# Opening of a two-layer encoder kernel: all token tiles loaded at once, remainders shared between two engines, projections begun between the transpositions

## The chip, the cores and the metric

One core of a Trainium2 chip runs the whole program. Its engines work through lists of their own and meet only at semaphores: TensorE (PE in the rows, its weight loads PEld), VectorE (DVE), ScalarE (ACT), GpSimd (POOL), and SyncE (SP), which here only issues DMAs. The metric is the device time of one execution in microseconds, lower is better.

## What is computed

A sequence of 1024 tokens of width 1024 goes through two layers, each a norm, a mixer and a residual. The change lies in the first norm and the start of the first projection:

```python
def rms_norm(x, g):
    xf = x.astype(jnp.float32)
    y = xf * lax.rsqrt(jnp.mean(xf * xf, axis=-1, keepdims=True) + EPS)
    return (y * g.astype(jnp.float32)).astype(x.dtype)

def attention_mixer(hn, w_in, sink, w_out):
    proj = hn @ w_in
    ...
    o = windowed_gqa_sink(q, k, v, sink)
    o = (o * jax.nn.silu(gate.astype(jnp.float32))).astype(hn.dtype)
    return o @ w_out

def reference(x, attn_norm, attn_w_in, ...):
    ...
    for i in range(DEPTH):
        p = layer_params[i]
        hn = rms_norm(x, p[0])
        if i % N_MIXERS == 0:
            x = x + attention_mixer(hn, *p[1:])
        else:
            x = x + deltanet_mixer(hn, *p[1:])
    return rms_norm(x, final_norm)
```

Everything is float32. The kernel gets near that precision with a rounded type: each operand is a rounded part (`_hi`) and a remainder (`_lo`), and a product is three matmuls, hi by hi, hi by lo and lo by hi.

## The kernel before

**Tokens** are cut into eight tiles of 128 (`NT`), the width into eight slices of 128 (`KT`). A token tile t goes through a chain over four engines, and `layer0_order` names its steps:

- `sq`: ScalarE squares the tile and sums the squares (L1037). It writes the squares into `xn`, a double buffer, so it waits until the transpositions of tile t-2, which used the same buffer, are done (`xT_done`).
- `nrm`: VectorE forms the mean (L1306), ScalarE takes the root (L1044), VectorE takes the reciprocal and multiplies the tile by it (L1308, L1309).
- `ntr`: TensorE transposes it in two halves of four 128x128 pieces into banks 4 and 5 (even t) or 6 and 7 (odd t) (L1750).
- `nout`: VectorE multiplies each half by the norm's weights into `hn_plain` (L1317).
- `nhi`: ScalarE rounds it into `hn_hi` (L1050).
- `nlo`: GpSimd subtracts, into `hn_lo` (L949).

**Weight tiles** of the projection (128 columns of `w_in`, 512 KB each) come into `ring0`; `rnd` rounds one on ScalarE (L1072), `split` forms its remainder on GpSimd (L955).

**Projections.** Tokens are taken in two halves of 512. An item `proj` is one slice of the width for one weight tile and one half: three matmuls of 128x512 (L1765). The first 16 items (48 matmuls) are two weight tiles on the first half, token tiles 0 to 3. The first of them waits until eight `nlo` are done (`hn_done`) and the first remainder is there; item 17, which works on the second half, waits for all sixteen. From then on the projections of the first layer run between the attention blocks, in one long stream.

**What sets the order.** `layer0_order` writes one list by hand (`AEV`), and each engine runs those of its events in that order, one after the other. An event that waits holds up everything behind it on its engine. `fill(n)` puts the next n projection items at that place. Before the change the loop of L375 puts tile t's `sq`, `nrm`, `ntr`, then `nout` of tile t-1, then `nhi` and `nlo` of tile t-2; four items stand between the transpositions of tiles 6 and 7 and the other twelve behind those of tile 7.

**Loads.** `xr` holds three token tiles (`XR`), so SyncE waits from tile 3 on until a buffer has been read (L810 to L829).

Of the kernel before, what the change touches and what calls it, by code (L numbers as in the profile page):

```python
# [21 lines left out]
F32 = mybir.dt.float32  # L22
F32R = mybir.dt.float32r
I32 = mybir.dt.int32
ALU = mybir.AluOpType
ACT = mybir.ActivationFunctionType
AX = mybir.AxisListType

P = 128
SEQ, D = 1024, 1024  # L30
NT = SEQ // P
# [16 lines left out]
XR = 3  # L48


def hybrid_encoder_kernel(nc, x, w0, wout0, w1, wba, wout1, norm0, norm1, normf, sink, convw, alog, dtb, onorm, out):
    ctx = ExitStack()
    with ctx:
# [7 lines left out]
        ident = sb("ident", [P, P])  # L61
        g0 = sb("g0", [P, KT])
# [60 lines left out]
        xr = take([XR, D])  # L123
# [14 lines left out]
        def hn_part(t, hf):  # L138
            return hn_f[:, 4 * hf:4 * hf + 4, t * P:(t + 1) * P]
# [207 lines left out]
        def layer0_order():  # L347
# [18 lines left out]
            def fill(n):  # L366
                for _ in range(min(n, len(stream))):
                    put(*stream.pop(0))
# [5 lines left out]
            stream += first + rest  # L374
            for t in range(NT):  # L375
                put(("sq", 0, t), ("nrm", 0, t), ("ntr", 0, t, 0), ("ntr", 0, t, 1))
                if t >= 1:
                    put(("nout", 0, t - 1, 0), ("nout", 0, t - 1, 1))
                if t >= 2:
                    for hf in range(2):  # L380
                        put(("nhi", 0, t - 2, hf), ("nlo", 0, t - 2, hf))
                if t < 2:
                    put(("rnd", t), ("split", t))
                if t >= 6:
                    fill(4 if t == 6 else 0)
            put(("nout", 0, NT - 1, 0), ("nout", 0, NT - 1, 1))
            for t in (NT - 2, NT - 1):
                for hf in range(2):
                    put(("nhi", 0, t, hf), ("nlo", 0, t, hf))
            put(("dist",))  # L390
# [106 lines left out]
        def xr_of(layer, t):  # L497

            if layer == 0:
                return xr[:, t % XR]  # L500
            return xr[:, (OP_SEQ.index((0, t)) if t < XR else NT + t - XR) % XR]
# [24 lines left out]
        def wout_lo(j):  # L526

            if j < 4:
                return hn_lo[:, 2 * j:2 * j + 2, 0:HALF]
            return wout_late_lo[:, j - 4].rearrange("p (f n) -> p f n", f=2)  # L530

        AEV = layer0_order()
# [271 lines left out]
        def _(sp):  # L804

            sp.dma_start(g0[:], norm0).then_inc(ld_g0, 16)
            for t in range(2):
                sp.dma_start(xr[:, t, :], x[:, t, :]).then_inc(ld_x[t], 16)
            sp.dma_start(ring0[:, 0], w0[0, 0]).then_inc(ld_w[0], 16)
            sp.dma_start(xr[:, 2, :], x[:, 2, :]).then_inc(ld_x[2], 16)  # L810
            sp.dma_start(ring0[:, 1], w0[0, 1]).then_inc(ld_w[1], 16)
            for t in range(XR, NT):
                sp.wait_ge(xn_done, t - XR + 1)
                sp.dma_start(xr[:, t % XR, :], x[:, t, :]).then_inc(ld_x[t], 16)
                if t == XR:
                    sp.dma_start(sinkb, sink.partition_broadcast(P)).then_inc(ld_small, 16)
                    sp.dma_start(wba_s, wba).then_inc(ld_small, 16)
                    sp.dma_start(g1[:], norm1).then_inc(ld_small, 16)
                    sp.dma_start(onw[:], onorm).then_inc(ld_small, 16)
                    sp.dma_start(cw[:], convw).then_inc(ld_small, 16)  # L820
                    sp.dma_start(alb[:], alog.partition_broadcast(P)).then_inc(ld_small, 16)
                    sp.dma_start(dtbb[:], dtb.partition_broadcast(P)).then_inc(ld_small, 16)
                if t == XR + 1:
                    for i in range(2):
                        sp.wait_ge(w0_split, i + 1)
                        sp.dma_start(ring0[:, i], w0[0, 2 + i]).then_inc(ld_w[i], 16)
            for tile in range(4, A_GROUPS * W0_TILES):
# [99 lines left out]
        def _(pool):  # L927
# [14 lines left out]
            for e in AEV:  # L942
                if e[0] == "nlo":

                    layer, t, hf = e[1:]
                    q = 2 * (NT * layer + t) + hf
                    tok, ks = slice(t * P, (t + 1) * P), slice(4 * hf, 4 * hf + 4)
                    pool.wait_ge(hi_done, q + 1)
                    gp.tensor_tensor(hn_lo[:, ks, tok], hn_part(t, hf), hn_hi[:, ks, tok].bitcast(F32),  # L949
                                     ALU.subtract).then_inc(hn_done, 1)  # L950
                elif e[0] == "split":

# [70 lines left out]
        def _(act):  # L1023
            sc = nc.scalar

            for e in AEV:
                if e[0] == "sq":
# [259 lines left out]
        def _(dve):  # L1287
# [12 lines left out]
            for e in AEV:  # L1300
                if e[0] == "nrm":

                    layer, t = e[1:]
                    n = NT * layer + t
                    dve.wait_ge(sq_done, n + 1)
                    ve.tensor_scalar(stat[:, 1, t:t + 1], stat[:, 0, t:t + 1], 1.0 / D, EPS, ALU.mult, ALU.add).then_inc(ms_done, 1)  # L1306
                    dve.wait_ge(rt_done, n + 1)
                    link(ve.reciprocal(stat[:, 2, t:t + 1], stat[:, 2, t:t + 1]))  # L1308
                    ve.tensor_scalar(xn_of[layer][:, t % 2], xr_of(layer, t), stat[:, 2, t:t + 1], None, ALU.mult).then_inc(xn_done, 1)  # L1309
                elif e[0] == "nout":  # L1310

# [828 lines left out]
```

## Time and profile before

| | us |
|---|---|
| median of 3 runs | 1339.96 |
| lowest, highest | 1338.75, 1340.84 |
| the profiled execution | 1342.17 |
| its span in the trace | 1340.5 |
| TensorE busy in the span | 1270.4 (95%) |

The span runs from the first to the last instruction in the trace; the execution's own time is 1.67 us longer, and lies 2.21 us above the median of the three runs. A row of the timeline gives the start and the duration of a group of instructions that follow each other, then engine, line, operation, output<-input and the count, and in brackets how long the engine sat idle before it and what released it. The page prints TensorE's granted clock as full over the opening; at which of its two levels (1.2 and 2.4 GHz) it ran is seen better in how far apart the starts of equal matmuls are.

### The profile page before, as it was taken

The page shows a single profiled execution, that of the slowest core. Times are in us where ns is not written, and L with a number is a line of the kernel's source. Part 1 is how long each engine was busy: PE and PEld are TensorE (multiplying, and loading weights), DVE is VectorE, ACT ScalarE, POOL GpSimd, SP SyncE. Part 2 cuts the span into 40 slices and gives each one's busy share as a digit, 9 for nine tenths or more (in the row PEclk, how much of TensorE's full clock was granted, in tenths as well). Part 3 has the DMA queues.
Part 4 walks back from the last instruction along what each step waited for, and adds up shares of the span by engine and source line. Part 5 has one row for each costly group of instructions (what it writes and reads, how often), then busy time and mean ns, then how long its engine had stood idle before and what let it go on. Part 6 is the DMA issues. An engine that isn't in the chain of part 4 may idle for free.

```text
span 1340.5 us, 23647 instructions
## 1 busy us (share of the span) xinstructions
PE 1270.4 (95%) x8829; PEld 973.2 (73%) x8829; DVE 852.6 (64%) x2340; ACT 691.8 (52%) x1806; POOL 278.3 (21%) x188
## 2 busy tenths in 40 slices
PE   5999999999999999878999999999999999998997
PEld 4866766666667776667888888888888888865643
DVE  5334545444656545786897978879788797852343
ACT  6245465464564444535557485574856647552121
POOL 7220111020232244204104031040310403100000
PEclk9999999999999989888999999999999999999999
DMA  5111101011322231111011111110201101053111
GB/s 195 33 32 32 33 32 32 17 32 64 126 69 89 79 126 64 49 33 49 32 33 64 33 52 45 53 60 17 79 18 65 48 18 64 1 221 110 48 68 74
DMA packets 21761, 79.94 MB, mean 60 GB/s; under 512 B 3216, under 2 KB 3472, under 8 KB 20240
## 3 DMA queue, kind: packets, MB, share of 16 engines
q1 hardware_dynamic: 21648, 78.42, 17.0%
q8 instruction: 72, 1.18, 0.4%
q14 instruction: 41, 0.34, 0.1%
HBM read 63.66 MB, written 14.75 MB: 58 GB/s over the span
## 4 chain that ended last, share of the span: by engine, by line
PE 75%; DVE 11%; ACT 9%; issue 2%; DMA 2%; SPq 0%; POOL 0%; DVEq 0%; POOLq 0%
PE bank L1865 19%; PE bank L1765 17%; PE bank L1841 6%; PE bank L1905 4%; PE bank L1880 4%; PE bank L1792 4%; DVE arena L1504 3%; PE bank L1803 3%; PE bank L1818 3%; PE bank L1957 2%; PE bank L1964 2%; PE bank L1990 2%; PE bank L1938 2%; PE bank L1939 2%; PE bank L1950 2%
## 5 line engine op out<-in xcount | busy, mean ns | idle before, releaser
L1865 PE MATMUL bank<-hn_hi,w_hi 128*128 128x512 f32 x512 | 222.5, 435 | 0.5 <-ACT arena L1147 0.5
L1865 PE MATMUL bank<-hn_hi,w_lo 128*128 128x512 f32 x512 | 202.5, 395 | 0.0
L1865 PE MATMUL bank<-hn_lo,w_hi 128*128 128x512 f32 x512 | 201.4, 393 | 0.0
L1765 PE MATMUL bank<-hn_hi,w_hi 128*128 128x512 f32 x320 | 137.0, 428 | 0.5 <-ACT arena L1082 0.2
L1765 PE MATMUL bank<-hn_hi,w_lo 128*128 128x512 f32 x320 | 126.1, 394 | 0.0
L1765 PE MATMUL bank<-hn_lo,w_hi 128*128 128x512 f32 x320 | 125.8, 393 | 0.0
L1003 POOL TENSOR_TENSOR w_lo<-arena,w_hi 128x1024 fp32r<-128x1024 f32 x24 | 59.9, 2495 | 301.6 <-ACT w_hi L1178 301.6
L1113 ACT ACTIVATE arena<-bank 128x512 f32<-128x512 f32 x88 | 52.2, 598 | 118.0 <-PE bank L1803 118.0
L1865 PEld LDWEIGHTS bank<-hn_hi,w_lo 128*128 128x128 f32 x512 | 96.8, 189 | 22.1
L1363 DVE CUSTOM_DVE_ANT_0 arena<-bank,arena 128x384 f32<-128x384 f32 (+1 forms) x128 | 70.1, 581 | 63.7 <-issue 63.4
L1865 PEld LDWEIGHTS bank<-hn_hi,w_hi 128*128 128x128 f32 x512 | 97.6, 191 | 16.2 <-ACT arena L1147 0.7
L1865 PEld LDWEIGHTS bank<-hn_lo,w_hi 128*128 128x128 f32 x512 | 98.0, 191 | 12.4
L955 POOL TENSOR_TENSOR w_lo<-arena,w_hi 128x1024 fp32r<-128x1024 f32 x20 | 48.0, 2399 | 266.7 <-ACT w_hi L1072 266.6
L1504 DVE SCALAR_TENSOR_TENSOR arena<-arena,cw 128x1024 f32<-128x1024 f32 x72 | 101.8, 1413 | 1.2
L1765 PEld LDWEIGHTS bank<-hn_hi,w_hi 128*128 128x128 f32 x320 | 60.7, 190 | 32.2 <-issue 22.8
L1104 ACT ACTIVATE arena<-arena 128x384 f32<-128x384 f32 (+1 forms) x128 | 73.5, 578 | 1.6 <-DVE arena L1372 1.4
L1164 ACT ACTIVATE arena<-bank,arena 128x128 f32<-128x128 f32 x112 | 41.4, 370 | 62.8 <-PE bank L1950 62.8
L1765 PEld LDWEIGHTS bank<-hn_hi,w_lo 128*128 128x128 f32 x320 | 60.5, 189 | 13.2
L1478 DVE SCALAR_TENSOR_TENSOR arena<-bank,arena 128x128 f32<-128x128 f32 x256 | 68.1, 341 | 2.0 <-ACT arena L1190 1.7
L1765 PEld LDWEIGHTS bank<-hn_lo,w_hi 128*128 128x128 f32 x320 | 61.0, 191 | 8.4
L1880 PE MATMUL bank<-arena 128*128 128x512 f32 x120 | 59.5, 624 | 5.7 <-DVE arena L1602 2.9
L1382 DVE TENSOR_SCALAR arena<-arena 128x384 f32<-128x384 f32 (+1 forms) x128 | 60.4, 536 | 1.1
(258 smaller groups left out, 2744.4 us busy)
## 6 DMA issues: line engine op xcount, KB each, us to landing
arena<-in_w SPq DMA_DIRECT2D x52, 512.0 KB, 3.5
arena<-in_x SPq DMA_DIRECT2D x16, 512.0 KB, 4.6
arena<-gc_scratch SPq DMA_DIRECT2D x8, 1024.0 KB, 4.8
x_scratch<-arena SPq DMA_DIRECT2D x13, 512.0 KB, 2.6
arena<-x_scratch SPq DMA_DIRECT2D x13, 512.0 KB, 3.5
out<-arena SPq DMA_DIRECT2D x8, 512.0 KB, 2.6
oT_scratch<-arena SPq DMA_DIRECT2D x7, 512.0 KB, 5.3
arena<-oT_scratch SPq DMA_DIRECT2D x7, 512.0 KB, 7.8
```

Source lines behind the costliest of these rows:

```text
L1003: gp.tensor_tensor(w_lo[:, t % 2], ring1[:, t % 2], w_hi[:, t % 2].bitcast(F32), ALU.subtract).then_inc(w_split, 1)
L1104: sc.activation(pr[:, sl, 0:w], pr[:, sl, 0:w], ACT.Exp, bias=small0[:, HPG + hd:HPG + hd + 1], accum_out=small0[:, 3 * HPG + hd:3 * HPG + ...
L1363: ve.tensor_tensor_reduce(out=pr[:, sl, 0:w], in0=s_bank(hd)[:, 0:w], in1=bias[:, hd, off:off + w], scale=1.0, scalar=small0[:, 7 * HPG + ...
L1382: ve.tensor_scalar(pr[:, sl, 0:w], pr[:, sl, 0:w], small0[:, 5 * HPG + hd:5 * HPG + hd + 1], None, ALU.mult).then_inc(p_norm, 1)
L1478: ins = ve.scalar_tensor_tensor(wq[:, d, c, part], bank_of[:, cc * P:(cc + 1) * P], head_tab2[:, h % 2, 7, u:u + 1], ET[:, d, c], ALU.mult ...
L1504: link(ve.scalar_tensor_tensor(dst, src, tap, dst, ALU.mult, ALU.add))
L1765: ins = te.matmul(bank[r % 2][:], wp[:, tile % 2, k], hp[:, k, hf * HALF:(hf + 1) * HALF], start=(k == 0 and m == 0), stop=(k == KT - 1 an ...
L1792: te.matmul(s_bank(hd)[:, 0:P * len(kt)], qT[rows, g % 2, pair, n * P:(n + 1) * P], kz[g % 2][rows, kt[0] * P:(kt[-1] + 1) * P], start=Tru ...
L1841: ins = te.matmul(bank[u % 2][:], op, wp, start=(j == 4 * part and m == 0), stop=(j == 4 * part + 3 and m == 2))
L1865: ins = te.matmul(b[:], wp[:, t % 2, k], hp[:, k, hf * HALF:(hf + 1) * HALF], start=(k == 0 and m == 0), stop=(k == KT - 1 and m == 2))
L1880: ins = te.matmul(bank[u % 2][:], oT_e[:, j, t * P:(t + 1) * P], wout_e[:, j, hf * HALF:(hf + 1) * HALF], start=(j == 0), stop=(j == FIN_H ...
L1905: ins = te.matmul(fin_bank(w)[:], oT_e[:, j, t * P:(t + 1) * P], wout_e[:, j, hf * HALF:(hf + 1) * HALF], start=(j == first), stop=(j == K ...
```

## The change

- **Loads:** SyncE issues all eight token tiles at the start without waits, tiles 0 and 1 first, then the norm's weights and the first weight tile, tiles 2 and 3, the second weight tile, tiles 4 to 7. Tiles 3 to 7 lie in `oT`, which is not in use yet. The small tables follow, then the third and fourth weight tile.
- **Order:** the hand-written list of the opening is new. `sq` of tiles 2 and 3 stand ahead of `nout` of tiles 0 and 1; tiles 2 and 3 get `nout`, `nhi`, `nlo` directly; three projection items then stand ahead of the transpositions of tile 4, two ahead of tile 5's, one each ahead of tile 6's and 7's. From tile 4 on `nhi` and `nlo` of tile t-1 stand directly behind its `nout`, ahead of `sq` of tile t+1.
- **Remainders:** VectorE does the remainders of the first two weight tiles and of the second halves of tiles 2 and 3; GpSimd keeps the other fourteen `nlo`. Ahead of its seventh it waits for all eight of the first half.
- **Mean:** on VectorE the step of L1306 follows `sq` in the list instead of opening `nrm`, so it stands ahead of `nout`.
- **Root table:** ScalarE takes a root of a constant first.

```diff
+            for t in range(2):
+                put(("sq", 0, t), ("nrm", 0, t), *two("ntr", t))
+            put(("sq", 0, 2), ("rnd", 0), *two("nout", 0), ("nrm", 0, 2), *two("ntr", 2), *two("nhi", 0), *two("nlo", 0))
+            put(("sq", 0, 3), *two("nout", 1), ("nrm", 0, 3), *two("ntr", 3), *two("nhi", 1), *two("nlo", 1), ("split", 0))
+            put(("sq", 0, 4))
+            for t in (2, 3):
+                put(*two("nout", t), *two("nhi", t), *two("nlo", t))
+            put(("rnd", 1), ("nrm", 0, 4), ("split", 1))
+            fill(3)
+            put(*two("ntr", 4))
+            for t in range(5, NT):
+                put(("sq", 0, t), ("nrm", 0, t))
+                fill(2 if t == 5 else 1)
+                put(*two("ntr", t), *two("nout", t - 1), *two("nhi", t - 1), *two("nlo", t - 1))
+            put(*two("nout", NT - 1), *two("nhi", NT - 1), *two("nlo", NT - 1))
...
             if layer == 0:
-                return xr[:, t % XR]
+                return xr[:, t] if t < XR else oT[:, t - XR]
...
+        def lo_by_dve(layer, t, hf):
+
+            return layer == 0 and t in (2, 3) and hf == 1
...
+            for t in range(NT):
+                sp.dma_start(xr_of(0, t), x[:, t, :]).then_inc(ld_x[t], 16)
+                if t == 1:
+                    sp.dma_start(g0[:], norm0).then_inc(ld_g0, 16)
+                    sp.dma_start(ring0[:, 0], w0[0, 0]).then_inc(ld_w[0], 16)
+                if t == 3:
+                    sp.dma_start(ring0[:, 1], w0[0, 1]).then_inc(ld_w[1], 16)
...
                     pool.wait_ge(hi_done, q + 1)
+                    if q == NT:
+                        pool.wait_ge(hn_done, NT)
...
-                elif e[0] == "split":
+                elif e[0] == "split" and e[1] >= 2:
...
+            act.wait_ge(consts, 1)
+            sc.activation(stat[:, 5, 0:1], ident[:, 0:1], ACT.Sqrt)
...
-                if e[0] == "nrm":
+                if e[0] == "sq" and e[1] == 0 or e[0] == "nrm" and e[1] == 1:
...
+                elif e[0] == "split" and e[1] < 2:
```

VectorE from the reciprocal of tile 3 on. Before the change (each row an instruction of L1306 to L1317):

```order
L1308 RECIPROCAL stat<-stat 128x1 [waits rt_done]
L1309 TENSOR_SCALAR arena<-arena,stat 128x1024 [waits dch]
L1317 TENSOR_TENSOR hn_plain_51<-bank4,g0 128x4x128 [waits xT_done]
L1317 TENSOR_TENSOR hn_plain_51<-bank5,g0 128x4x128 [waits xT_done]
L1306 TENSOR_SCALAR stat<-stat 128x1 [waits sq_done]
```

And with it, where L1332 is the weight remainder, L1340 `nout` and L1326 the remainder of a half tile:

```order
L1319 RECIPROCAL stat<-stat 128x1 [waits rt_done]
L1320 TENSOR_SCALAR arena<-arena,stat 128x1024 [waits dch]
L1332 TENSOR_TENSOR w0_lo_53<-arena,w0_hi_52 128x1024 [waits w0_rounded]
L1313 TENSOR_SCALAR stat<-stat 128x1 [waits sq_done]
L1340 TENSOR_TENSOR hn_plain_51<-bank4,g0 128x4x128 [waits xT_done]
L1340 TENSOR_TENSOR hn_plain_51<-bank5,g0 128x4x128 [waits xT_done]
L1326 TENSOR_TENSOR hn_lo_50<-hn_plain_51,hn_hi_49 128x4x128 [waits hi_done]
L1340 TENSOR_TENSOR hn_plain_51<-bank6,g0 128x4x128 [waits xT_done]
L1340 TENSOR_TENSOR hn_plain_51<-bank7,g0 128x4x128 [waits xT_done]
L1326 TENSOR_TENSOR hn_lo_50<-hn_plain_51,hn_hi_49 128x4x128 [waits hi_done]
```

Three subtractions have come in between the multiplication of tile 3 and the end of tile 3's `nout`, and the mean of tile 4 stands ahead of tile 2's `nout`.

ScalarE for tiles 5 to 7 before the change, where L1037 is `sq`, L1044 the root and L1050 `nhi` (two halves each, the last row six halves):

```order
L1037 ACTIVATE arena,stat<-arena 128x1024 [waits xT_done,ld_x6]
L1044 ACTIVATE stat<-stat 128x1 [waits ms_done]
L1050 ACTIVATE hn_hi_49<-hn_plain_51 128x4x128 [waits half_done] x2
L1037 ACTIVATE arena,stat<-arena 128x1024 [waits xT_done,ld_x7]
L1044 ACTIVATE stat<-stat 128x1 [waits ms_done]
L1050 ACTIVATE hn_hi_49<-hn_plain_51 128x4x128 [waits half_done] x6
```

And with it (L1044, L1051 and L1057 are the same three steps):

```order
L1044 ACTIVATE arena,stat<-arena 128x1024 [waits xT_done,ld_x6]
L1051 ACTIVATE stat<-stat 128x1 [waits ms_done]
L1057 ACTIVATE hn_hi_49<-hn_plain_51 128x4x128 [waits half_done] x2
L1044 ACTIVATE arena,stat<-arena 128x1024 [waits xT_done,ld_x7]
L1051 ACTIVATE stat<-stat 128x1 [waits ms_done]
L1057 ACTIVATE hn_hi_49<-hn_plain_51 128x4x128 [waits half_done] x4
```

The rows look alike, but the two `nhi` ahead of `sq` of tile 7 are those of tile 4 before the change and those of tile 5 with it: six halves are left over at the end before, four with it.

TensorE with the change, from the first projection item to the transpositions of tile 6 (L1773 is a transposition, L1788 a projection):

```order
L1788 MATMUL bank0<-hn_hi_49,w0_hi_52 128x512 [waits hn_done,w0_split]
...
L1773 MATMUL bank4<-ident,arena 128x128 [waits half_done,xn_done]
L1773 MATMUL bank4<-ident,arena 128x128 x3
L1773 MATMUL bank5<-ident,arena 128x128 [waits half_done,xn_done]
L1773 MATMUL bank5<-ident,arena 128x128 x3
L1788 MATMUL bank0<-hn_hi_49,w0_hi_52 128x512
...
L1773 MATMUL bank6<-ident,arena 128x128 [waits half_done,xn_done]
L1773 MATMUL bank6<-ident,arena 128x128 x3
```

Before the change the first projection item stands behind the transpositions of tile 6, so that one tile is left to transpose behind it; now four are.

## Rows read from the trace of the kernel before

**Rows 1.** The page's first part: busy time and share of the span.
```profile
PE 1270.4 (95%) x8829; PEld 973.2 (73%) x8829; DVE 852.6 (64%) x2340; ACT 691.8 (52%) x1806; POOL 278.3 (21%) x188
```

**Rows 2.** Stages: window, length, then each engine's busy time (count), clock, DMA share, GB/s.
```profile
0.00:28.49 28.49, 13.41 (x57) 11.04 (x57) 17.20 (x51) 20.20 (x39) 21.22 (x22) 1.00 0.68 229
28.49:42.27 13.78, 13.78 (x58) 11.35 (x57) 8.48 (x13) 3.91 (x7) 8.83 (x7) 1.00 0.01 2
```

**Rows 3.** Timeline of TensorE around the first projection items.
```profile
26.87 1.97 PE L1750 MATMUL bank<-ident,arena 128*128 128x128 f32 x8 [0.94 <-DVE arena L1309]
28.49 0.78 PE L1765 MATMUL bank<-hn_hi,w_hi 128*128 128x512 f32 x1
...
32.05 0.63 PE L1765 MATMUL bank<-hn_hi,w_lo 128*128 128x512 f32 x1
...
33.29 1.04 PE L1750 MATMUL bank<-ident,arena 128*128 128x128 f32 x8
```

**Rows 4.** The chain that ended last, its longest pieces: start, duration, what.
```profile
34.33 13.63 PE bank L1765 x60
```

**Rows 5.** Timeline of tile 5's norm; last, tile 7 on its way to GpSimd.
```profile
21.34 1.06 ACT L1037 ACTIVATE arena<-arena 128x1024 f32<-128x1024 f32 x1 [1.31 <-DMA arena<-in_x]
...
22.53 0.15 DVE L1306 TENSOR_SCALAR stat<-stat 128x1 f32<-128x1 f32 x1 [0.92 <-ACT arena L1037]
...
23.15 0.75 DVE L1309 TENSOR_SCALAR arena<-arena,stat 128x1024 f32<-128x1024 f32 x1
...
23.96 1.97 PE L1750 MATMUL bank<-ident,arena 128*128 128x128 f32 x8 [1.53 <-DVE arena L1309]
...
33.93 1.29 DVE L1317 TENSOR_TENSOR hn_plain<-bank,g 128x512 f32<-128x512 f32 x2 [3.00 <-PE bank L1750]
...
34.66 1.23 ACT L1050 ACTIVATE hn_hi<-hn_plain 128x512 fp32r<-128x512 f32 x2 [3.06 <-DVE hn_plain L1317]
```

**Rows 6.** Timeline: SyncE's first token load; ScalarE's table load in tile 0.
```profile
1.23 0.89 SPq L808 DMA_DIRECT2D arena<-in_x  x2
...
6.14 1.28 ACT L1044 ACT_TABLE_LOAD   x1
```

**Rows 7.** DMA issues between 1.1 and 1.5 us: count, size, us to landing.
```profile
arena<-in_x SPq DMA_DIRECT2D x1, 512.0 KB, 3.7
```

**Rows 8.** The same between 3.0 and 3.4 us, the fifth large load.
```profile
arena<-in_w SPq DMA_DIRECT2D x1, 512.0 KB, 7.1
```

**Rows 9.** Timeline of VectorE beside GpSimd's remainders, tile 3 and tile 7.
```profile
16.30 1.19 DVE L1309 TENSOR_SCALAR arena<-arena,stat 128x1024 f32<-128x1024 f32 x1
...
16.90 1.73 POOL L949 TENSOR_TENSOR hn_lo<-hn_plain,hn_hi 128x512 fp32r<-128x512 f32 x1
...
35.37 1.29 POOL L949 TENSOR_TENSOR hn_lo<-hn_plain,hn_hi 128x512 fp32r<-128x512 f32 x1 [0.76 <-ACT hn_hi L1050]
...
35.45 1.48 DVE L1323 TENSOR_TENSOR wba_lo<-arena,wba_hi 128x256 fp32r<-128x256 f32 x1
```

**Rows 10.** Groups of VectorE by shape: busy us, mean ns, idle before.
```profile
L1581 DVE TENSOR_TENSOR arena<-arena 128x512 f32<-128x512 f32 x16 | 10.3, 688 | 11.7 <-ACT arena L1237 11.7
L1511 DVE TENSOR_TENSOR w_lo<-arena,w_hi 128x1024 fp32r<-128x1024 f32 x6 | 7.1, 1182 | 0.0
```

**Rows 11.** Timeline of TensorE behind three of its idle gaps later in the program.
```profile
378.75 0.33 PE L1803 MATMUL bank<-ident,arena 128*128 128x128 f32 x1 [1.74 <-DVE arena L1382]
...
379.39 0.39 PE L1841 MATMUL bank<-hn_lo,oT_hi 128*128 128x512 f32 x1
...
477.19 0.79 PE L1841 MATMUL bank<-w_hi,oT_hi 128*128 128x512 f32 x1 [3.09 <-DVE arena L1401]
...
478.63 0.63 PE L1841 MATMUL bank<-w_hi,oT_hi 128*128 128x512 f32 x1
...
1192.30 4.51 PE L1880 MATMUL bank<-arena 128*128 128x512 f32 x6 [2.80 <-DMA arena<-oT_scratch]
...
1197.81 1.98 PE L1880 MATMUL bank<-arena 128*128 128x512 f32 x4
```

More of the change, by code:

```diff
@@ L374, in layer0_order, with two @@
             stream += first + rest
[L375 to L389, printed above, removed]
+            def two(what, t):
+                return [(what, 0, t, hf) for hf in range(2)]
+            for t in range(2):
[13 more added lines that the diff above has]
+            put(*two("nout", NT - 1), *two("nhi", NT - 1), *two("nlo", NT - 1))
             put(("dist",))
@@ L804, in _ @@
         def _(sp):
[L806 to L826, printed above, removed]
@@ new lines, in _ @@
+            for t in range(NT):
[5 more added lines that the diff above has]
+                    sp.dma_start(ring0[:, 1], w0[0, 1]).then_inc(ld_w[1], 16)
+            sp.dma_start(sinkb, sink.partition_broadcast(P)).then_inc(ld_small, 16)
+            sp.dma_start(wba_s, wba).then_inc(ld_small, 16)
@@ new lines, in _ @@
+            sp.dma_start(g1[:], norm1).then_inc(ld_small, 16)
+            sp.dma_start(onw[:], onorm).then_inc(ld_small, 16)
+            sp.dma_start(cw[:], convw).then_inc(ld_small, 16)
+            sp.dma_start(alb[:], alog.partition_broadcast(P)).then_inc(ld_small, 16)
+            sp.dma_start(dtbb[:], dtb.partition_broadcast(P)).then_inc(ld_small, 16)
+            for i in range(2):
+                sp.wait_ge(w0_split, i + 1)
+                sp.dma_start(ring0[:, i], w0[0, 2 + i]).then_inc(ld_w[i], 16)
@@ L942, in _ @@
             for e in AEV:
-                if e[0] == "nlo":
+                if e[0] == "nlo" and not lo_by_dve(*e[1:]):
                     layer, t, hf = e[1:]
@@ L1306, in _ @@
                     ve.tensor_scalar(stat[:, 1, t:t + 1], stat[:, 0, t:t + 1], 1.0 / D, EPS, ALU.mult, ALU.add).then_inc(ms_done, 1)
+                if e[0] == "nrm":
+                    layer, t = e[1:]
+                    n = NT * layer + t
                     dve.wait_ge(rt_done, n + 1)
@@ L1309, in _ @@
                     ve.tensor_scalar(xn_of[layer][:, t % 2], xr_of(layer, t), stat[:, 2, t:t + 1], None, ALU.mult).then_inc(xn_done, 1)
+                elif e[0] == "nlo" and lo_by_dve(*e[1:]):
+                    layer, t, hf = e[1:]
+                    tok, ks = slice(t * P, (t + 1) * P), slice(4 * hf, 4 * hf + 4)
+                    dve.wait_ge(hi_done, 2 * t + hf + 1)
+                    ve.tensor_tensor(hn_lo[:, ks, tok], hn_part(t, hf), hn_hi[:, ks, tok].bitcast(F32),
+                                     ALU.subtract).then_inc(hn_done, 1)
+                elif e[0] == "split" and e[1] < 2:
+                    tile = e[1]
+                    dve.wait_ge(w0_rounded, tile + 1)
+                    ve.tensor_tensor(w0_lo[:, tile], ring0[:, tile], w0_hi[:, tile].bitcast(F32), ALU.subtract).then_inc(w0_split, 1)
                 elif e[0] == "nout":
```

## Prediction, written before the changed kernel ran

> **What bounds the kernel now.** I read the page first: TensorE is busy for 95% of the span [rows 1], so whatever it loses or gains is the kernel's time. Then the stages: up to its first projection matmul at 28.49 us TensorE is busy for only 13.41 us, from there on without a gap [rows 2]. The opening is thus worth looking at, and two moments matter. The first is the start of the projections, S: 28.49. The second is the end of the first 48 matmuls (16 items), E. Behind E the order is the same in both kernels, so the change is worth what E moves, as long as the second half of the tokens is ready by then. In the timeline [rows 3] the reader sees eight transpositions (tile 6), then matmuls whose records last 0.63 us, up to 32.05, then eight transpositions in 1.04 us instead of 1.97 (tile 7). The chain of waits shows 60 matmuls in 13.63 us, 0.227 each [rows 4]. So TensorE is at its lower level (1.2 GHz) at first, though the page prints the granted clock as 1.00 there: the 12 matmuls and the way to tile 7's transpositions take 33.29 - 28.49 = 4.8 us, 0.40 each, where 12 x 0.227 = 2.7 would do. The piece of 60 begins at 34.33 with the second matmul behind tile 7, so that E = 34.33 + 35 x 0.227 = 42.3, or S + 13.8.
>
> What E must cover is easily counted: 48 matmuls x 0.227 = 10.9, plus about 2 for the slow beginning, plus 1.0 for each tile that is still to be transposed behind S. Before, that is one tile; with the change it is four. So even without any wait E = S + 17: **the change has to bring S forward by 3 us only to break even.** The second view to read is then the chain of a tile, step by step [rows 5].
>
> **The chain of a tile.** From `sq` to the first transposition: 21.34 to 22.53 (square to mean), to 23.15 (root, reciprocal), to 23.96: 2.6 us. From there the transpositions need about 1.1 us (at the lower level) until VectorE can begin `nout` of the first half. From `nout` to `nhi` is 34.66 - 33.93 = 0.73, and ScalarE is free again after the two `nhi`, 1.2 later. GpSimd's subtraction begins 35.37 - 34.66 = 0.71 after `nhi` [rows 5, 9].
>
> **Part 1, the start S.** The loads first. The first token tile was issued at 1.23 and landed 3.7 later, at 4.9 [rows 6, 7]; the fifth large load, issued at about 3.1, landed 7.1 later, at 10.2 [rows 8]: four transfers of 512 KB in 5.3 us, 1.3 each. With the change the first is issued at about 0.80, in the place of the norm's weights, and lands at 4.5; the ten large loads then land in their order every 1.3 us, the last near 16.3. No tile from the second on is waited for by my count, so the loads give 0.4. The table load of 1.28 that stands in tile 0's chain [rows 6] is done while ScalarE waits for tile 0. Together tile 0's multiplication ends at 4.5 + 2.6 = 7.1 instead of 8.6.
>
> From there I replay the four engines' lists with the durations above:
> - tile 0 is transposed from 7.1 to 8.9, tile 1 to 10.3; `sq` of tile 2 can start at 9.0, since it needs tile 0's buffer. VectorE has nothing to do from 8.6 to 10.2, because the mean of tile 2 now stands ahead of tile 0's `nout`, ready since 8.3. Then `nout` of tile 0 (2 x 0.6), and tile 2's multiplication ends at 12.5. Before, it ended at 14.6: 2.1 gained.
> - `sq` of tile 3 starts at 12.3, VectorE again waits for it until 13.5, does `nout` of tile 1, and starts tile 3's multiplication at 15.1; it ends at 15.8.
> - now the subtractions on VectorE. Alone they cost 1.18 for a weight tile and 0.69 for a half tile [rows 10]. Beside GpSimd they cost more: the subtraction of 256 columns at 35.45 took 1.48 us, and it ended just 0.27 after GpSimd's of 35.37 had (35.37 + 1.29 = 36.66); a multiplication that takes 0.75 alone took 1.19 there, and GpSimd's next, 1.73 instead of 1.27 [rows 5, 9]. I take it that the one that starts first makes the other wait for nearly its whole length. GpSimd starts the remainder of tile 1 when VectorE's multiplication ends, so the weight remainder waits for about 1.0 and ends at 17.95.
> - mean of tile 4, `nout` of tile 2 from 18.05; `nhi`; GpSimd has the first half from 19.5 to 20.7, VectorE's half waits for that until 20.5 and ends at 21.2; the same for tile 3: `nout` from 21.15, GpSimd 22.6 to 23.8, VectorE to 24.3. Eight remainders are there, and S = 24.4 to 24.5, **4.0 us ahead of 28.49**.
>
> So four remainders taken from GpSimd pay for themselves, but of the about 3.7 us that they cost VectorE alone (2 x 1.18 + 2 x 0.69) a part and 2.0 us of waiting stand in front of S.
>
> **Part 2, from S to E.** Three items at the lower level (the ninth matmul started 3.56 after the first [rows 3]) take about 3.8, then tile 4 is transposed at S + 3.8 = 28.2. From here on the new order binds. `sq` of tile 6 stands behind `nhi` of tile 4 on ScalarE, and that one needs tile 4's transpositions: 1.1 (to `nout`) + 0.73 + 1.2 = 3.0, then 2.6 to the transpositions of tile 6: 28.2 + 5.6 = 33.9. `nout` of tile 5 stands behind tile 6's multiplication on VectorE, then `nhi` of tile 5, then `sq` of tile 7: 1.9 + 2.6, less 0.1 that overlaps, 4.4: tile 7's transpositions start at 38.3. Before, a tile came every 2.9 us there (23.96, 26.87), because `nhi` of the tile two back was long ready when its turn came. TensorE has only one item between tiles 6 and 7, 0.7 us, and so it stands idle for 4.4 - 1.0 - 0.7 = 2.7 us ahead of tile 7, and for 1.3 ahead of tile 6. Behind tile 7 come its 1.0 and nine items of 3 x 0.227: 7.1. E = 38.3 + 7.1 = 45.4 if TensorE stays at the higher level.
>
> Does it? After a gap of 1.74 the matmul record behind lasts 0.39; after 3.09 it is 0.63, and after 2.80 six matmuls take 4.51, 0.75 each, where 0.50 is usual a little later (4 in 1.98) [rows 11]. The gap of 2.7 is nearest to the one of 2.80, so I take the lower level again. That costs what it cost at the start, 4.8 - 2.7 - 0.2 for the seam = 1.9, here rounded down to 1.8, since the transpositions are part of it: **E = 47.2 instead of 42.3, +4.9 us.**
>
> GpSimd ends its sixteenth remainder at about 44.5, 0.9 ahead of E even in the faster case, so the second half is not waited for. The loads of the third and fourth weight tile wait for the remainders at 18.0 and 26.3 and are used much later; the copies behind `dist` on VectorE have several us of room. They cost nothing; if GpSimd were over 2.7 us later, item 17 would wait for it.
>
> **The sum.** S -4.0; three more tiles behind S, +3.1 (3 x 1.04); waits of TensorE between the items, 1.3 + 2.7 = 4.0; the second slow stretch +1.8. Together +4.9. The profiled execution's 1340.5 would be 1345.4 in its span; the runs' median is 1339.96, so 1344.9.
>
> **Rivals.**
> 1. *TensorE keeps the higher level over the gap.* For it: the gap of 1.74 did. Then +3.1, 1343.1.
> 2. *VectorE loses the race at tile 3.* Its multiplication is ready at 15.07 and GpSimd's first remainder of tile 1 at 15.08 by my count, a tie. If GpSimd is first, the multiplication waits for 1.1 and all behind it moves: +6.0, 1346.0. The rows show such waits in both directions [rows 9]. The Trainium skill says it as a rule (SBUF — State Buffer, "Who interferes with whom"): issue order decides which of the two blocks, and the other blocks fully. By that rule the tie at tile 3 is worth the 1.1, and the rows agree.
> 3. *The subtractions on VectorE do not wait for GpSimd.* The only such row is one of 256 columns. Without any waits my replay has S at 22.5 and all behind it 2.0 sooner. With the slow stretch E is +2.9, without it +1.1: **no measurable change**, 1341.1. It decides itself at tile 7's transpositions: they must start before about 37.9 for E to stay within 2.7 of 42.3 at the higher level.
> 4. *The tiles come at their old pace of 2.9.* Then tile 7 starts at 28.2 + 8.7 = 36.9 and E = 44.0, +1.7, no measurable change. Against it stands ScalarE's list. Rivals 3 and 4 together would give 42.1, no gain either: for a clear gain S would have to be under 22.
>
> **How the numbers follow.** A difference of 0.2% (2.7 us) is about what a measurement of this kernel can tell from none. Forecast as worked out 0.38; rival 1 0.20; rival 2 (with or without the second slow stretch) 0.14; rival 3 0.12; rival 4 0.10; something faster that the rows do not show, an earlier S by over 3 us, 0.06. Rivals 3 and 4 and a little of rival 1, which lies just over the bound, make no measurable change: 0.25. Faster 0.06, slower 0.69. The range goes from rival 3 without the slow stretch to rival 2 with it and a little: 1340.8 to 1346.8.
>
> **What would show it.** First projection matmul near 24.5. VectorE's weight remainder at about 2.2 us, two thirds of it waiting. TensorE's transpositions of tiles 4, 6, 7 near 28.2, 33.9 and 38.3, with a gap of about 2.7 ahead of the last and records of 0.63 behind it; item 17 near 47.2. If tile 7 comes at 36 or sooner, my reading of ScalarE's order is wrong; if S comes after 26, it is the waits between VectorE and GpSimd or the loads.

## Result and profile of the changed kernel

| | before | changed |
|---|---|---|
| median | 1339.81 us (4 runs, 1338.75 to 1340.84) | 1347.93 us (4 runs, 1347.44 to 1348.56) |
| span of the first trace | 1340.5 | 1345.7 |
| first projection matmul, S | 28.5 | 25.8 |
| tile 7 transposed from | 33.3 | 39.9 |
| end of the first 48 matmuls, E | 42.3 | 46.9 |

The change makes the kernel slower: 1.0061 times the time before, 95% interval 1.0043 to 1.0078, 8.1 us by the medians. The direction was forecast, the size was not: 1344.9 was forecast, with a range up to 1346.8. Two executions were slow and stand in no ratio, one of 1786.4 us in the run without VectorE's help and one of 1444.5 us in the run with the mean moved back (mean granted clock 0.84, elsewhere 0.98 to 0.99), whose trace is for this reason read only up to S.

E is read here from a row that every trace has: the first transposition of the values (L1777 before, L1800 changed) starts 24 matmuls behind E, 5.5 us later. Read so, E is the start of item 17 to within 0.1 us (47.00 in this trace), and where TensorE waits ahead of item 17 the wait is in it.

TensorE in the changed kernel, timeline (start, duration, engine, line, operation, count, idle before):

```profile
25.84 0.77 PE L1788 MATMUL bank<-hn_hi,w_hi 128*128 128x512 f32 x1 [6.70 <-DVE hn_lo L1326]
...
29.82 1.74 PE L1773 MATMUL bank<-ident,arena 128*128 128x128 f32 x8
...
35.49 1.09 PE L1773 MATMUL bank<-ident,arena 128*128 128x128 f32 x8 [0.97 <-DVE arena L1320]
...
39.89 1.09 PE L1773 MATMUL bank<-ident,arena 128*128 128x128 f32 x8 [2.59 <-DVE arena L1320]
...
41.06 0.39 PE L1788 MATMUL bank<-hn_lo,w_hi 128*128 128x512 f32 x1
...
52.44 0.60 PE L1800 MATMUL bank<-ident,arena 128*128 128x128 f32 x4
```

These answer to [rows 3]. The start came 2.65 us sooner, but tiles 4 to 7 are transposed behind it, at 29.8, 32.8, 35.5 and 39.9, where before only tile 7 was left. Ahead of tiles 6 and 7 TensorE stands idle for 0.97 and 2.59 us; before, it had no gap between 28.5 and 42.3. Behind the gap the records last 0.39 us: in this execution TensorE stayed at its higher level (2.4 GHz).

The stages as in [rows 2], of the changed kernel (each engine's busy time with its count, then granted clock, DMA share, GB/s):

```profile
0.00:28.49 28.49, 9.31 (x38) 7.85 (x39) 17.75 (x46) 15.55 (x30) 10.84 (x16) 0.75 0.60 211
28.49:42.27 13.78, 10.22 (x55) 8.24 (x54) 7.76 (x16) 6.78 (x14) 6.14 (x5) 0.90 0.12 39
```

In the window that was full before (13.78 us busy), TensorE now works for 10.22. GpSimd's work is halved up to 28.49 (10.84 against 21.22 us), and still S comes only 2.65 us sooner.

VectorE, ScalarE and GpSimd on the way to S, timeline of the changed kernel, which answers to [rows 5, 9, 10]:

```profile
9.51 1.06 ACT L1044 ACTIVATE arena<-arena 128x1024 f32<-128x1024 f32 x1 [1.83 <-DMA arena<-in_x]
...
10.69 0.15 DVE L1313 TENSOR_SCALAR stat<-stat 128x1 f32<-128x1 f32 x1 [2.03 <-ACT arena L1044]
...
15.26 1.86 DVE L1320 TENSOR_SCALAR arena<-arena,stat 128x1024 f32<-128x1024 f32 x1
...
15.30 2.94 POOL L954 TENSOR_TENSOR hn_lo<-hn_plain,hn_hi 128x512 fp32r<-128x512 f32 x2
...
16.53 1.72 POOL L954 TENSOR_TENSOR hn_lo<-hn_plain,hn_hi 128x512 fp32r<-128x512 f32 x1
...
17.04 2.28 DVE L1332 TENSOR_TENSOR w_lo<-arena,w_hi 128x1024 fp32r<-128x1024 f32 x1
...
21.28 1.26 DVE L1326 TENSOR_TENSOR hn_lo<-hn_plain,hn_hi 128x512 fp32r<-128x512 f32 x1 [0.70 <-ACT hn_hi L1057]
...
24.43 1.27 DVE L1326 TENSOR_TENSOR hn_lo<-hn_plain,hn_hi 128x512 fp32r<-128x512 f32 x1 [0.69 <-ACT hn_hi L1057]
```

The row of 15.30 holds two subtractions, and that of 16.53 is the second of them. VectorE waits 2.03 us for the squares of tile 2 while tile 0's multiplication by the norm's weights is ready. Its multiplication of tile 3 takes 1.86 instead of 0.75 us, the weight remainder 2.28 instead of 1.18, each half tile 1.27 instead of 0.69: together 3.4 us more than alone, beside GpSimd's subtractions. Of VectorE's three subtractions two stand between the multiplication of tile 3 and the end of tile 3's `nout`, and the third behind it; the section on the change puts all three in between.

The loads, DMA issues from 0.7 to 1.0 us and from 2.6 to 2.8 (count, size, us to landing), for [rows 7, 8]:

```profile
arena<-in_x SPq DMA_DIRECT2D x1, 512.0 KB, 3.8
```

```profile
arena<-in_x SPq DMA_DIRECT2D x1, 512.0 KB, 6.8
```

Tile 2 lands at 9.4 to 9.5, 1.0 us later than my one every 1.3 us from 4.5 on would have it, and ScalarE's squares wait for it here.

### The profile page after: what moved, and what is told of

The parts are those of the page before. It is cut to its first block, busy times and chain, and to the rows that moved or that the text cites. A ratio compares the mean times of both kernels' runs of the same rounds, so it can differ in the third digit from the quotient of the medians.

```text
span 1345.7 us, 23648 instructions
## 1 busy us (share of the span) xinstructions
PE 1267.4 (94%) x8829; PEld 970.1 (72%) x8829; DVE 856.9 (64%) x2344; ACT 691.3 (51%) x1806; POOL 269.5 (20%) x184
## 3 DMA queue, kind: packets, MB, share of 16 engines
q8 instruction: 72, 1.18, 0.4%
## 4 chain that ended last, share of the span: by engine, by line
PE 74%; DVE 12%; ACT 9%; issue 2%; DMA 1%; SPq 0%; POOL 0%; DVEq 0%; POOLq 0%; ACTq 0%
PE bank L1888 19%; PE bank L1788 16%; PE bank L1864 5%; PE bank L1928 4%; PE bank L1903 4%; PE bank L1815 4%; DVE arena L1527 3%; PE bank L1841 3%; PE bank L1826 3%; PE bank L1980 2%; PE bank L1987 2%; PE bank L2013 2%; PE bank L1962 2%; PE bank L1961 2%; PE bank L1973 2%
## 5 line engine op out<-in xcount | busy, mean ns | idle before, releaser
L1788 PE MATMUL bank<-hn_hi,w_hi 128*128 128x512 f32 x320 | 137.2, 429 | 7.2 <-DVE hn_lo L1326 6.7
L1788 PE MATMUL bank<-hn_hi,w_lo 128*128 128x512 f32 x320 | 126.1, 394 | 0.0
L1788 PE MATMUL bank<-hn_lo,w_hi 128*128 128x512 f32 x320 | 125.8, 393 | 0.0
L1008 POOL TENSOR_TENSOR w_lo<-arena,w_hi 128x1024 fp32r<-128x1024 f32 x24 | 59.8, 2492 | 301.7 <-ACT w_hi L1185 301.7
L960 POOL TENSOR_TENSOR w_lo<-arena,w_hi 128x1024 fp32r<-128x1024 f32 x18 | 42.9, 2385 | 257.3 <-ACT w_hi L1079 257.3
L1788 PEld LDWEIGHTS bank<-hn_hi,w_hi 128*128 128x128 f32 x320 | 60.6, 189 | 39.0 <-issue 29.9
L1171 ACT ACTIVATE arena<-bank,arena 128x128 f32<-128x128 f32 x112 | 41.4, 370 | 62.9 <-PE bank L1973 62.9
L1788 PEld LDWEIGHTS bank<-hn_hi,w_lo 128*128 128x128 f32 x320 | 60.5, 189 | 13.3
L1788 PEld LDWEIGHTS bank<-hn_lo,w_hi 128*128 128x128 f32 x320 | 60.8, 190 | 8.2
```

Source lines behind the costliest of these rows:

```text
L1008: gp.tensor_tensor(w_lo[:, t % 2], ring1[:, t % 2], w_hi[:, t % 2].bitcast(F32), ALU.subtract).then_inc(w_split, 1)
L1788: ins = te.matmul(bank[r % 2][:], wp[:, tile % 2, k], hp[:, k, hf * HALF:(hf + 1) * HALF], start=(k == 0 and m == 0), stop=(k == KT - 1 an ...
```

## Experiments

Each kernel was compared with runs of the kernel before on the same chip. Ratios carry a 95% interval.

**The kernel before, again.** No edit.

> The kernel before, unchanged, once more, for a second trace and more times. The changed kernel was 8.1 us slower by the medians, but only 5.2 by the two spans (1345.7 against 1340.5), and the profiled execution of the kernel before was 2.2 above its median. Theory 1 (the whole loss is in the opening, and the first trace of before was a slow execution by chance): this trace has a span near 1338 to 1339, the first matmul at 28.5 and the end of the 48 matmuls at 42.3 as before, and it is shorter somewhere behind the opening, by about 2. Theory 2 (the times of before scatter, the traces do not): span 1340.5 again, and the median moves up towards 1341.

Measured: ratio 0.9995 (0.9986 to 1.0004), median 1339.45 us. TensorE in this trace:

```profile
32.34 1.03 PE L1750 MATMUL bank<-ident,arena 128*128 128x128 f32 x8
...
46.88 0.60 PE L1777 MATMUL bank<-ident,arena 128*128 128x128 f32 x4
```

The span is 1338.6. The first matmul came at 28.1 and tile 7 at 32.3 instead of 33.3: 0.4 us from S, 0.6 from a shorter slow beginning (4.22 instead of 4.80 us from S to tile 7). E is 41.4, not 42.3. Of the 1.9 us that the spans differ, 0.9 lie in the opening and 1.1 between 456 and 487 us. So neither theory is quite right: the first trace was long in part in the opening itself, and two executions of one kernel differ there by 0.9. From here on the kernel before has E = 41.4 to 42.3.

**The changed kernel, again.** No edit, two more traces.

> The changed kernel, unchanged, once more. Theory 1 (the opening costs 4.7 us, since the 48 matmuls end at 47.0 instead of 42.3, and all else is the same): 4 to 5.5 us slower than before in runs of the same chip. Theory 2 (something behind the opening costs 3 us more, which the two traces do not show): 7 to 9 us slower again. First matmul again near 25.8 if VectorE always loses to GpSimd at tile 3, near 24.8 if that is a tie that falls either way.

> The changed kernel unchanged, a third trace. In two traces the opening cost 4.7 and 6.6 us against traces of the kernel before, the medians differ by 7.3 to 8.1. Theory (a gap of 2.6 us ahead of tile 7's transpositions is followed by TensorE's lower level in most executions, the first trace was an exception): records of 0.63 us behind it, end of the 48 matmuls near 48, 6 to 8 us slower. Rival (the rest lies behind the opening): end near 47 and a stretch behind it longer than in the kernel before.

Measured: ratio 1.0055 (1.0042 to 1.0067), median 1347.13 us, and 1.0056 (1.004 to 1.0072), 1349.0 us. TensorE in the second trace, then in the third:

```profile
39.32 1.24 PE L1773 MATMUL bank<-ident,arena 128*128 128x128 f32 x8 [2.61 <-DVE arena L1320]
...
42.06 0.63 PE L1788 MATMUL bank<-hn_lo,w_hi 128*128 128x512 f32 x1
...
53.47 0.60 PE L1800 MATMUL bank<-ident,arena 128*128 128x128 f32 x4
```

```profile
39.76 1.22 PE L1773 MATMUL bank<-ident,arena 128*128 128x128 f32 x8 [2.60 <-DVE arena L1320]
...
42.48 0.63 PE L1788 MATMUL bank<-hn_lo,w_hi 128*128 128x512 f32 x1
...
53.90 0.60 PE L1800 MATMUL bank<-ident,arena 128*128 128x128 f32 x4
```

The same gap, 2.59, 2.61 and 2.60 us, and two outcomes: records of 0.39 behind it in the first trace, 0.63 up to about 43.5 in the other two. The granted clock from 38 to 46 us says the same, 1.00 in the first, 0.75 to 0.82 in the others. The gap ahead of tile 6 was not quite equal, 0.97 in the first and 1.19 and 1.21 in the others; whether that decides is not shown. From tile 7 to E it takes 7.0 us in the first, 8.6 in the others: the second slow stretch costs 1.6. E is 46.9, 48.0 and 48.4. Against 41.4 and 42.3 the opening costs 4.6 to 7.0 us, 5.9 on average; the three timings say 8.1, 7.0 and 8.5 by medians of few runs, and their intervals reach down to 5.4 to 5.8. Tile 3's multiplication took 1.86 us in all three, and 1.85 or 1.86 in the three variants below that do not touch it (tail order, all token remainders on GpSimd, gap filled). So this was no tie that falls either way: VectorE lost every time.

**The order of the tail undone.** Rounding and remainder of tiles 4 to 7 one tile later in the list, as before the change.

```diff
-                put(*two("ntr", t), *two("nout", t - 1), *two("nhi", t - 1), *two("nlo", t - 1))
+                put(*two("ntr", t), *two("nout", t - 1))
+                if t >= 6:
+                    put(*two("nhi", t - 2), *two("nlo", t - 2))
...
```

> The changed kernel with one part undone: from tile 4 on, the rounding and the remainder of a tile stand one tile later in the list again, as before the change, so that ScalarE squares tiles 6 and 7 without waiting for the tile just transposed. Theory 1 (ScalarE's order sets the pace of tiles 6 and 7, 4.4 us each): first matmul at 25.8 as in the changed kernel, tile 7 transposed near 37.0 instead of 39.9, end of the 48 matmuls near 44.3, and 2.7 us faster than the changed kernel. Rival (the pace is set by VectorE or by TensorE's own items between the transpositions): tile 7 stays within 1 us of 39.9 and the time within 1 us of the changed kernel.

Measured: ratio 1.0033 (1.002 to 1.0046), 1343.92 us. TensorE:

```profile
37.03 1.09 PE L1777 MATMUL bank<-ident,arena 128*128 128x128 f32 x8 [1.09 <-DVE arena L1324]
...
45.02 0.47 PE L1792 MATMUL bank<-hn_hi,w_hi 128*128 128x512 f32 x1 [0.75 <-POOL hn_lo L958]
```

First matmul at 25.66, tile 7 at 37.03: 2.3 to 2.9 us sooner, as the theory had it. ScalarE's order set the pace: tile 7 now comes 2.8 us behind tile 6 (34.21), not 4.4. The gap is 1.09 us, and no slow records follow. At E, TensorE now waits 0.75 us for GpSimd's last remainder: a bound that the changed kernel hides stands right behind. E is 45.0, where 44.3 was expected. The median is 3.2 us below that of the changed kernel measured beside it, nearly half of the 7.0 that the change costs there; the two intervals just overlap.

**All token remainders on GpSimd.** `lo_by_dve` returns False, and GpSimd's wait goes.

> The changed kernel with GpSimd doing all sixteen remainders of the tokens again (VectorE keeps the two weight remainders), and without GpSimd's wait ahead of its ninth. Theory 1 (VectorE's half tiles wait for GpSimd and so save little): first matmul 0.6 us later than in the changed kernel, near 26.4, and as much slower, within what can be measured. Rival (the waits cost more than the sharing saves): first matmul at 25.3 or sooner.

Measured: ratio 1.006 (1.0048 to 1.0073), 1347.72 us. First matmul at 26.47, 0.9 us after that of the run beside it (25.61), E = 48.9. But half of that stands already at tile 3's multiplication (15.46 against 15.02), ahead of the first shared half tile, and against the third trace of the changed kernel, where it began at 15.43, S is 0.45 later. The sharing of the half tiles is worth about 0.4 us of S, and the rival falls; by time the two cannot be told apart. The gap ahead of tile 7 is 2.58 us, and the slow stretch follows here too.

**The mean behind the multiplication again.**

```diff
-                if e[0] == "sq" and e[1] == 0 or e[0] == "nrm" and e[1] == 1:
+                if e[0] == "nrm":
```

> The changed kernel with one part undone: the mean of a tile (VectorE, after ScalarE's squares) stands behind the previous tile's multiplication by the norm's weights again. In the changed kernel VectorE waits for the squares of tiles 2 and 3 while that multiplication is ready, and then loses tile 3's race against GpSimd by about 0.2 us. Theory (the mean's place costs up to 1.9 us of the start): first matmul near 24.1 instead of 25.6 to 25.8, tile 7 transposed near 38.0 instead of 39.3 to 39.9, end of the 48 matmuls near 45.1, or 46.7 with a second slow stretch of TensorE; 1.5 to 1.9 us faster than the changed kernel. Rival (VectorE meets GpSimd at another place instead): first matmul at 25 or later, no difference.

Measured: ratio 1.0045 (1.0032 to 1.0059). VectorE:

```profile
14.59 1.16 DVE L1320 TENSOR_SCALAR arena<-arena,stat 128x1024 f32<-128x1024 f32 x1
```

Tile 3's multiplication took 1.16 us instead of 1.86, and the first matmul came at 24.42. That is 1.2 to 1.6 us sooner than in the changed kernel: the mean's place does cost about that much of S, through VectorE's wait (the multiplication begins at 14.59 instead of 15.0 to 15.4) and the lost race. In the time a gain of that size is within the noise: the ratio is 0.0010 to 0.0016 below those of the changed kernel, and the intervals overlap.

**The gap ahead of tile 7 filled.** `fill` puts four items there instead of one.

```diff
-                fill(2 if t == 5 else 1)
+                fill({5: 2, 6: 1, 7: 4}[t])
```

> The changed kernel with one number changed: four projection items instead of one between the transpositions of tiles 6 and 7, so that TensorE has work in its gap of 2.6 us there. The tiles' chain is untouched. Theory (a gap of 2.6 us sends TensorE to its lower level in some executions, 1.6 us each time, and the idle time itself is worth little, since the last remainder ends near 46): first matmul 25.7, tile 7 at 39.3 to 39.9 as before, gap under 0.8 us, no records of 0.63 us behind it, end of the 48 matmuls near 46.1; 0.8 us faster than the changed kernel's better executions, 2.4 than its others, so about 2 by the medians. Rival (the clock has no part in it): 0.8 us faster at most.

Measured: ratio 1.0056 (1.0043 to 1.0069), 1347.58 us, not faster. TensorE:

```profile
40.40 1.09 PE L1773 MATMUL bank<-ident,arena 128*128 128x128 f32 x8 [0.59 <-DVE arena L1320]
...
47.20 0.47 PE L1788 MATMUL bank<-hn_hi,w_hi 128*128 128x512 f32 x1 [1.60 <-POOL hn_lo L954]
```

The gap is down to 0.59 and no slow records follow, as expected; since one trace of the changed kernel had none either, one trace does not prove that filling removes them. And the time is handed back. S was 26.18 in this execution and tile 7 came at 40.4; and since TensorE is done sooner, it waits 1.60 us for GpSimd's sixteenth remainder. E = 47.2, 0.8 to 1.2 us under the two traces of the changed kernel with the slow stretch, and the timing shows none of it. So the tiles' chain, which ends in that remainder, bounds E almost as tightly as TensorE does: in the first trace of the changed kernel that remainder ended at 46.6, 0.4 ahead of item 17.

**Only the loads.** The kernel before with the change's SyncE part and `xr_of`.

> The kernel before with only the loads of the change: all token tiles issued at the start, without waits. Theory (loads were no limit before, except for one wait of 1.3 us at tile 5, and the first weight tile now lands 0.6 us later, which holds up ScalarE's second tile since its rounding stands ahead): first matmul at 28.8, end of the 48 matmuls 0 to 1 us later than before (42.3 or 41.4 in two traces), time the same within 0.1%. Rival (the waits of the loads were what held the opening): first matmul at 27 or sooner and 1 us or more faster.

Measured: ratio 1.0007 (0.9998 to 1.0017). TensorE, and ScalarE, which waits for the first weight tile ahead of tile 1's squares:

```profile
12.41 1.97 PE L1746 MATMUL bank<-ident,arena 128*128 128x128 f32 x8 [2.25 <-DVE arena L1305]
...
47.43 0.60 PE L1773 MATMUL bank<-ident,arena 128*128 128x128 f32 x4
```

```profile
8.25 1.06 ACT L1068 ACTIVATE w_hi<-arena 128x1024 fp32r<-128x1024 f32 x1 [1.16 <-DMA arena<-in_w]
9.22 1.04 ACT L1033 ACTIVATE arena<-arena 128x1024 f32<-128x1024 f32 x1
```

First matmul at 29.37, E = 41.9. The loads alone bring nothing: what they save is lost while ScalarE waits for the weight tile with the next token tile already there, and again, for 1.23 us, for the second. S is 0.9 to 1.3 us later than before, and E is not, because only two records of 0.63 us follow S here, against five and eight in the two traces of the kernel before.

**The order of before with the rest of the change.** Loads, root table, mean and weight remainders as in the change; one half tile (tile 3) on VectorE; roundings of the weights later:

```diff
+            for t in range(NT):
+                put(("sq", 0, t), ("nrm", 0, t))
+                fill({6: 2, 7: 4}.get(t, 0))
+                put(*two("ntr", t))
+                if t >= 1:
+                    put(*two("nout", t - 1))
+                if t >= 2:
+                    for hf in range(2):
+                        put(("nhi", 0, t - 2, hf), ("nlo", 0, t - 2, hf))
+                if t in (1, 5):
+                    put(("rnd", t // 4), ("split", t // 4))
...
```

> Loads, root table, VectorE's weight remainders and mean of the changed kernel, but with the order of the kernel before (rounding and remainder two tiles behind), the rounding of the first weight tile behind tile 1 and of the second behind tile 5, two projection items ahead of tile 6's transpositions and four ahead of tile 7's, and one half tile (tile 3) on VectorE. Theory (what cost time in the change is the order alone, and the loads and the sharing are worth something when the tiles keep their pace of 2.9 us): first matmul near 23.0, tile 7 at 29.8, end of the 48 matmuls near 37.7, 4 to 5 us faster than the kernel before, near 1335. Rival (the engines collide in any order): end at 41 or later, no gain.

Measured: ratio 0.9967 (0.9955 to 0.9979), 1335.24 us: **faster than both kernels**, 4.4 us by the ratio. TensorE:

```profile
21.44 1.97 PE L1773 MATMUL bank<-ident,arena 128*128 128x128 f32 x8 [0.95 <-DVE arena L1320]
23.32 0.77 PE L1788 MATMUL bank<-hn_hi,w_hi 128*128 128x512 f32 x1
...
25.65 1.10 PE L1773 MATMUL bank<-ident,arena 128*128 128x128 f32 x8
...
29.37 1.03 PE L1773 MATMUL bank<-ident,arena 128*128 128x128 f32 x8
...
42.51 0.60 PE L1800 MATMUL bank<-ident,arena 128*128 128x128 f32 x4
```

S = 23.3 with only two tiles left to transpose, no gap behind it, E = 37.0. That is 4.4 to 5.3 us ahead of the kernel before, and the median follows it. Against the first trace of before, S is 5.2 sooner, one more tile behind it costs 1.0, and the slow beginning is 1.1 shorter (six matmuls in 2.33 us). The traced execution itself took 1339.6 us, the slowest of eight (the others 1334.4 to 1335.6); what it lost lies behind the opening. From the matmul that starts at 300.2 us in the first trace of before, it took 1042.9 us to the end, the two traces of before 1040.3 and 1039.3.

**That order without VectorE's help.** All remainders on GpSimd.

> The kernel of e8_order with GpSimd doing every remainder again, of tokens and weights; VectorE does none, all else as there. Theory (the order carries the gain of e8, the sharing between VectorE and GpSimd only a small part, since each makes the other wait): first matmul near 23.6 instead of 22.9, end of the 48 matmuls near 37.9, 0.9 us slower than e8 and still about 4 faster than the kernel before. Rival (the sharing carries the gain): first matmul at 26 or later, at most 1 us faster than the kernel before.

Measured: ratio 0.9978 (0.9967 to 0.999). First matmul at 23.51, E = 37.6, 0.6 us behind the kernel above. By the ratios 2.9 of the 4.4 us remain, with intervals that overlap. The theory holds: most of the gain needs no sharing.

**That order with the roundings behind tiles 0 and 1.** The edit is against the kernel of the order of before, with VectorE's help.

```diff
-                if t in (1, 5):
-                    put(("rnd", t // 4), ("split", t // 4))
+                if t < 2:
+                    put(("rnd", t), ("split", t))
```

> The kernel of e8_order with the rounding of the two weight tiles behind token tiles 0 and 1 again, as in the kernel before; VectorE keeps their remainders. Theory (ScalarE works in order, so that a rounding ahead of tile 1's squares waits for a weight tile that lands at 8.3 and pushes all tiles back): first matmul near 26.2, end of the 48 matmuls near 40.3, 3 us slower than e8 and about 2 faster than the kernel before. Rival (the place of the roundings is indifferent, the gain comes from the early loads and the projection items): within 1 us of e8.

Measured: ratio 0.9999 (0.999 to 1.0008), no gain left. TensorE:

```profile
11.98 1.97 PE L1773 MATMUL bank<-ident,arena 128*128 128x128 f32 x8 [2.86 <-DVE arena L1320]
...
26.50 0.77 PE L1788 MATMUL bank<-hn_hi,w_hi 128*128 128x512 f32 x1
...
45.30 0.60 PE L1800 MATMUL bank<-ident,arena 128*128 128x128 f32 x4
```

Tile 1 comes at 11.98, since its squares stand behind a rounding that waits 2.28 us for the load, and tile 2's stand behind the other, which waits 1.28; the first matmul is 3.2 us later, E = 39.8, 2.8 later. The place of the two roundings is what the early loads needed. E is still 1.6 to 2.5 us ahead of before, which the timing does not show. Behind the opening the traces scatter, whatever it does: the twelve whose whole length is read take 29.9 to 31.0 us for the stretch that lies from 456 to 487 us in the first trace, and 146.5 to 149.7 from the matmul at 1192.3 us there to the end.

## Why the prediction was right in direction and wrong in size

- **The balance** (more tiles behind S, so that S must come 3 us sooner to break even) held as arithmetic: S came 2.65 sooner in the first trace, which by itself makes 0.4 us of loss. The rest of the 4.6 to 7.0 by which E is later are TensorE's gaps and the slow stretch.
- **From S to tile 7** was forecast at 13.9 us; it took 14.05, 13.7 and 13.7 in the three traces. The gap was forecast at 2.7, measured at 2.6. The undone tail order shows the cause: ScalarE's list.
- **The clock behind the gap.** The slow stretch that I took as likeliest came in two traces of three, and with the same gap in the run with all remainders on GpSimd; it cost 1.6, forecast 1.8.
- **S was the step that failed.** "S = 24.4 to 24.5" was 25.8, 25.6 and 26.0, and the term that was wrong is the race at tile 3. I counted a tie, VectorE's multiplication ready at 15.07 and GpSimd's remainder at 15.08, and took it as won, ending at 15.8. It was ready at 15.26, 15.02 and 15.43, took 1.86 us each time instead of 0.75, and so cost 1.1 us every time, the greater part of the 1.2 to 1.6 by which S is late. It was no tie of two starts either: GpSimd's four subtractions of tiles 0 and 1 follow each other without a pause, from 12.37 to 18.25 in the first trace, and the multiplication, ready at 15.26 while the second of them ran, got in only near the end of the third. The loss stood as rival 2 with 0.14; all six traces of this order show it.
- **The loads** were sized wrong too, but weigh little. I let ten transfers land every 1.3 us from 4.5 on; the first weight tile, issued at 2.16, took 6.1 us, and tile 2 came at 9.4 instead of 8.4. ScalarE, though, could not begin tile 2's squares at 9.0 as I had it, load or no load: they wait for tile 0's transpositions, which end near 9.3. In the second trace, where these began at 7.22, that is what released them, 2.04 us later. By that measure the load held the squares up for 0.1, 0 and 0.4 us in the three traces. The row of the second:

```profile
9.26 1.06 ACT L1044 ACTIVATE arena<-arena 128x1024 f32<-128x1024 f32 x1 [1.71 <-PE bank L1773]
```

- VectorE's other waits were priced nearly right: the weight remainder 2.28 (forecast 2.2), the half tiles 1.27 (1.1 to 1.2 by the replay). The run with the mean moved back gave 1.2 to 1.6 us of S back.
- **The case that came** is rival 2 with the second slow stretch: 42.3 + 6.0 = 48.3 by the forecast, E = 48.0 and 48.4 in two traces of three. But its time, 1346.0, is still 1.9 under the first measured median. Of this 0.4 is the baseline: I worked from a trace of before with E = 42.3, and with the second, 41.4, the mean is 41.9. 48.2 - 41.9 = 6.3 us is what the opening costs in the two traces with the slow stretch. The rest of the miss, about 1.5 us, is not explained.
- **Rivals 3 and 4** fell: the subtractions do wait, and the pace was 4.4 us. The sentence that "for a clear gain S would have to be under 22" is right for this order only: with S = 23.3 and two tiles left instead of four, the gain is 4.4 us.
- **What stays open:** the three timings of the changed kernel (7.0 to 8.5 us) lie 1 to 2 us above the 6.3 of the opening. Their intervals contain it, and behind the opening the traces show no difference: from the same matmul at 300.2 us to the end it takes 1040.3 and 1039.3 us before, and 1040.8, 1037.7 and 1041.7 with the change. Whether there is more than scatter was not settled.

## What to carry to other kernels

Starting the bottleneck engine sooner is not enough in itself: count what must still be fed to it behind the start, and ask whether the producers keep their pace. A software pipeline in in-order lists lives on its distance: moving a step from two tiles behind to one tile behind turned 2.9 us per tile into 4.4, and moving it back gave 2.8. Where two instructions of engines that make each other wait come out as a tie by your count, price the loss in. And ahead of taking over work from a neighbour engine, look for a step in front of the chain that waits for a load: two roundings moved back, by one tile and by four, were worth 2.8 us of the opening, while sharing remainders with VectorE was worth 0.6 of it.

## What the runs showed of the hardware

- The same idle gap of TensorE, 2.58 to 2.61 us, is followed by the lower level (records of 0.63 us) in three traces and by the higher one (0.39 us) in a fourth. Gaps of 0.6 to 1.6 us between projection items never were followed by the lower one. What decides in the case of 2.6 us is not shown. Such a gap can thus make E scatter by 1.6 us from one execution to the next.
- The waits between VectorE and GpSimd cost nearly a whole instruction of the other: 1.27 instead of 0.69, 1.86 instead of 0.75, 2.28 instead of 1.18, and 1.72 instead of 1.27 on GpSimd. Beside GpSimd's remainder of a whole weight tile (a record of 2.38 us) a multiplication took 2.99 instead of 0.75, in the run without VectorE's help.
- The Trainium skill says that the shared port pair is held for the whole instruction and that issue order decides (SBUF — State Buffer, "Who interferes with whom"). On the length of the waits the trace agrees. On the order the records do not bear it out: VectorE's multiplication of tile 3 begins at 15.26, 0.04 us ahead of GpSimd's next subtraction at 15.30, and still waits for all of it. It ended at 17.12; if its work takes the usual 0.75 us it began at 16.37, 0.2 ahead of GpSimd's next record at 16.53, and that record is 0.45 longer than the usual 1.27. The profile's spans of GpSimd are rough, so starts this close do not tell who came first.
